# Low parts of weight chunks behind the maximum of a unit's scores, in a two-block transformer layer on one core

## The reference, cut to what matters

```
(qa, ka, va, qb, kb, vb, qc, kc, vc, qi, ki, wi, gates) = split(xn @ w_in[l])
o_a = chunk_band_attention(qa, ka, va, rel_bias_a[l])       # softmax(q k * scale + bias) v
o_b = diff_attention(rope(qb), rope(kb), vb, lam, ...)      # softmax(c=0) - lam * softmax(c=1)
o_c = dsa_attention(rope(qc), rope(kc), vc, index ..., topk)  # softmax over selected keys
g = sigmoid(gates).reshape(b, s, 3, D)
y = g[0] * (o_a @ w_up_a) + g[1] * (o_b @ w_up_b) + g[2] * (o_c @ w_up_c)
x = x + y @ w_out
```

## Time and profile before

| | |
|---|---|
| median of 3 runs | 1695.42 us (1692.92 to 1697.69) |
| the profiled execution | 1695.85 us, of which the recorded span is 1693.8 us |
| PE busy | 1603.3 us, 95% of the span |
| DVE busy | 876.6 us, 52% |
| ACT busy | 621.3 us, 37% |
| POOL busy | 58.1 us, 3% |
| mean granted TensorE clock | 0.975 of full speed |

### The profile page before, as it was taken

The page is one execution under the profiler, slowest core; times in us unless marked ns, Lnnn a source line. Parts: engine busy times, 40 slices in busy tenths (PEclk is TensorE's granted clock), DMA queues, the critical chain, the costliest instruction groups (busy, mean ns, idle before and its releaser), DMA issues.

```text
span 1693.8 us, 25178 instructions
## 1 busy us (share of the span) xinstructions
PE 1603.3 (95%) x10739; PEld 1285.8 (76%) x10739; DVE 876.6 (52%) x1272; ACT 621.3 (37%) x990; POOL 58.1 (3%) x28
## 2 busy tenths in 40 slices
PE   8898989889989999998999899999999899899998
PEld 7785434443434479897788799999988788799998
DVE  6933212121211287678555676647668755476653
ACT  2123202111211154545514544435454542464443
POOL 0000000000000000060000000000015000000000
PEclk9988999999999999999999899999999999999999
DMA  9156999999999985426222655474634424256550
GB/s 351 66 212 258 427 430 428 428 428 428 430 429 426 423 298 181 140 103 221 100 102 98 211 187 174 163 256 158 216 105 150 147 78 174 94 181 199 174 188 37
DMA packets 126912, 393.78 MB, mean 232 GB/s; under 512 B 4320, under 2 KB 60000, under 8 KB 114016
## 3 DMA queue, kind: packets, MB, share of 16 engines
q1 hardware_dynamic: 126816, 392.38, 61.2%
HBM read 386.34 MB, written 1.05 MB: 229 GB/s over the span
## 4 chain that ended last, share of the span: by engine, by line
PE 66%; DVE 15%; DMA 10%; ACT 5%; issue 3%; SPq 0%; DVEq 0%; ACTq 0%
PE psum L1240 10%; DMA ring<-w 9%; PE psum L973 7%; PE psum L974 7%; PE psum L976 7%; PE psum L1506 5%; PE psum L1305 3%; DVE outs L1949 2%; ACT wp L1592 2%; PE psum L1573 2%; PE psum L1576 2%; PE psum L1575 2%; PE psum L1203 2%; PE psum L1004 2%; DVE score L2347 1%
## 5 line engine op out<-in xcount | busy, mean ns | idle before, releaser
L973 PE MATMUL psum<-h_hi,w_hi 128*128 128x256 f32 x1456 | 366.6, 289 | 1.8 <-ACT outs L1595 1.4
L974 PE MATMUL psum<-h_hi,w_lo 128*128 128x256 f32 x1456 | 361.5, 285 | 0.0
L973 PEld LDWEIGHTS psum<-h_hi,w_hi 128*128 128x128 f32 x1456 | 282.3, 194 | 7.3 <-issue 5.1
L974 PEld LDWEIGHTS psum<-h_hi,w_lo 128*128 128x128 f32 x1456 | 282.7, 194 | 0.2
L624 DVE TENSOR_TENSOR w_lo<-raw_a,w_hi 128x1024 fp32r<-128x1024 f32 x170 | 204.9, 1223 | 136.0 <-ACT w_hi L1595 135.1
L1595 ACT ACTIVATE w_hi<-raw_a 128x1024 fp32r<-128x1024 f32 x186 | 193.1, 1053 | 186.0 <-PE psum L976 70.2
L976 PE MATMUL psum<-h_lo,w_hi 128*128 128x256 f32 x1456 | 205.0, 284 | 0.0
L1240 PE MATMUL psum<-ring,outs 128*64 128x512 f32 x720 | 166.0, 617 | 27.3 <-DMA ring<-w 26.1
L976 PEld LDWEIGHTS psum<-h_lo,w_hi 128*128 128x128 f32 x1456 | 188.8, 193 | 0.0
L1240 PEld LDWEIGHTS psum<-ring,outs 128*64 128x64 f32 x720 | 58.0, 142 | 132.7 <-issue 132.7
L624 DVE TENSOR_TENSOR w_lo<-raw_b,w_hi 128x1024 fp32r<-128x1024 f32 x84 | 101.7, 1223 | 60.4 <-ACT w_hi L1595 59.7
(11 more groups left out here) (298 smaller groups left out, 2516.4 us busy)
## 6 DMA issues: line engine op xcount, KB each, us to landing
ring<-w SPq DMA_DIRECT2D x76, 2048.0 KB, 16.6
raw_a<-w_in SPq DMA_DIRECT2D x20, 2048.0 KB, 8.2
raw_a<-w_gu SPq DMA_DIRECT2D x32, 1024.0 KB, 7.8
raw_b<-w_in SPq DMA_DIRECT2D x10, 2048.0 KB, 8.4
wp<-w SPq DMA_DIRECT2D x8, 2048.0 KB, 18.7
hs<-w SPq DMA_DIRECT2D x8, 2048.0 KB, 23.1
raw_b<-w_gu SPq DMA_DIRECT2D x12, 1024.0 KB, 7.5
raw_a<-w_down SPq DMA_DIRECT2D x8, 1536.0 KB, 6.6
```

What stands on the lines that cost most here:

```text
L973: mm(to, hi[:, k, :], h_hi[:, k, :], start=(k == 0), stop=False)
L974: mm(to, lo[:, k, :], h_hi[:, k, :], start=False, stop=False)
```

## The change

One condition in `with_splits`, the one that puts the collected low parts into the list:

```diff
@@ -230,7 +230,7 @@
         unit = unit or (w[0] == "rope" and w[1] >= 3)
         if unit:
             out.append(w)
-        if w[0] == "probs" or not unit:
+        if w[0] == "scores" or w in (("probs", 7), ("probs", 23), ("probs", 27)) or not unit:
             out += low
             low = []
         held = ...
```

## The result

The changed kernel takes 1676.63 us (median of 4 runs, 1675.84 to 1677.74) against 1694.29 us for the kernel before in the same comparison: ratio 0.9891, 95% interval 0.9875 to 0.9907. It is 17.7 us (1.1%) faster. The forecast was 1677.2 us.

The account below looks back on a forecast made before the run. PE was taken as the tightest engine, its gaps ended by work handed round through DVE and ACT. Stretch gains of 1.84, 3.32, 6.57 and 6.47 us sum to 18.2: 1695.42 - 18.2 = 1677.2 us, range 1672 to 1687.

Parts of the forecast that it names:

- What bounds: Units 2 to 7 and 9 to 23, both layers: PE has least room but isn't full, with 17.9 us of gaps.
- a circle through DVE and ACT: Unit steps: maximum, exponential, probabilities, low, evacuation, scaling, next maximum run one behind another and end PE's gaps, e.g. 1.81 us.
- The place left: Ahead of the scaling: next unit's scaling and maximum begin up to 1.14 us earlier, without split waits up to 1.27 us.
- A and C: Unit steps where PE waits for nothing: 4.45 us from even to odd, 4.65 us from odd to even.
- The place gone to: Between maximum and reciprocals: a low costs 0.06 us in odd, about 0.25 us in even units, which PE's slack takes.
- Expected leftovers: PE waits left per layer: 1.03 us at step 13, half of it at step 14, 0.2 us at step 4.
- ACT, loads, PE's demand for the lows: Split wait of 1.27 us goes; loads and PE's use of chunks, up to some 2.5 us later, cost nothing.
- Sum: Units 2 to 7 take 22.85 us, units 9 to 23 take 61.75 us, in both layers: 18.2 us gained.
- The clock: Four falls of PE's clock in the unit steps, 5.9 us of the 18.2, go because PE stands idle less.
- the rival in which the falls stay: Clock falls return at waits left at the start of B and the rotations: gain 12.3 us, 1683.1 us, chance 0.14.
- What passes on: Work behind the unit steps moves up, so the gain counts in full; otherwise the first two gains, 5.2 us, are lost.
- The rule on the busiest engine: Optimise the highest-occupancy engine first: read so, moving DVE's work has no effect, 1695.4 us, chance 0.04.

Follow-up runs that it names:

- late_ahead: Kernel before, with each low still ahead of the scores but put out one step later, when its split is done: 1679.33 us, ratio 0.9911 to before.
- no_low: Changed kernel without the low subtraction of chunks 30 to 34 and 50 to 62 in each layer: 1675.16 us, ratio 0.9882 to the kernel before.
- only_a: Kernel before with the change for units 0 to 7 alone (4 moved lows a layer): 1689.09 us against 1694.96, ratio 0.9962.
- only_bc: Kernel before with the change for units 8 to 23 alone (13 moved lows a layer): 1683.28 us against 1694.96, ratio 0.9931.
- rope_and_32: Changed kernel with rotations ahead of the scaling in steps 13 and 15 and low 32 behind unit 4's scores: 1675.36 us, ratio 0.9884 to before.
- before_again: Kernel before, no edit, profiled once more: 1696.12 us.
- after_again: Changed kernel, no edit, run once more: 1677.04 us against 1695.43 for the kernel before, ratio 0.9893.
- twice_behind: Changed kernel with each of 36 lows done twice behind the maximum: 1700.11 us, ratio 1.0031 to the kernel before.

## Why the prediction was right

**What bounds.** Right: PE with gaps, ended by a circle through DVE and ACT that held the low. With the low off it, the scaling waits for PE. One reading was wrong: "PE equally busy (34.65 us)" in both layers compares two stretches of 36.5 us that hold 283 and 270 matmuls. Over the same units PE was busy 22.84 and 24.32 us with the same gap of 1.85 us, so the 1.48 us are all clock, as the prediction concluded.

**The place left.** Right in sum, but it named two costs without weighing them, the low's own 1.14 us and the wait for its split. `late_ahead` weighs them: the wait alone, with what hangs on it, is 15.5 of the 18.2 us of the stretches, and all of it in A and C. My expectation for that kernel (10 to 13 us) still gave the low's own time too much.

**The place gone to.** Right: `no_low` shows that the moved lows cost next to nothing there but at three steps of a layer. Expected leftovers were 1.03 us, half of it and 0.2 us; they are 0.95, 0.47 and, by the stretch 22.92 against 22.65, 0.27 us.

**ACT, loads, PE's demand for the lows.** Right: in the four stretches after, none of PE's and DVE's waits is for a low, a split or a load.

**Sum.** 22.85 us expected for units 2 to 7 in both layers, 22.92 and 22.91 measured; 61.75 for 9 to 23, 61.66 and 61.68 measured. In the long one the step from unit 17 to 18 was put at 4.45 us, taken from A, and is 4.31. The gain of the stretches, 18.2 us, is the measured one.

**The clock.** That the four falls would go was right: the clock is 1.00 in all four stretches of both profiled executions. The 5.9 us put on them is too much. Without a fall the first stretch of the kernel before takes 24.69 us (its layer 0) and the long one 67.62 (`only_a`, layer 1), twice that is 184.62 us, and with the four falls it was 187.40. So the falls were worth 2.8 of the 18.2 us, and 15.4 are gaps that would have gone without any fall. By the same working the rival in which the falls stay would have cost less than the 5.9 us it was given. The sum wasn't touched by it, as it was made of whole stretches.

**What passes on.** Right: `only_a` and `only_bc` add up. The step left out is that the parts behind the units could change at all: between two executions of one kernel, and in layer 0 between kernels, they differ by 1 to 2 us with the clock in cross attention. That the forecast came out to 0.6 us is in part luck. The medians gained 17.7 us and not 18.2, and the median of before was 1.1 us lower this time (1694.29 against 1695.42), both within the scatter of the runs.

**The rule on the busiest engine.** The prediction set the advice of the Trainium skill ("Perfetto Trace Analysis", Identifying the Most-Contended Engine) to optimise the engine with the highest occupancy first against that of its next section, Optimization Strategy, to look for what blocks that engine in its gaps. The trace doesn't bear out the reading that work on another engine is worth nothing: DVE's order alone gave 17.7 us with DVE 52% busy. It agrees with the second: PE's waits in the four stretches before ended with DVE's probabilities.

## What to carry to other kernels

In a loop where engines hand work round, look on each in-order engine for the instruction that stands between a product and the operation that releases the next engine, and for the idle time behind that release: work which nobody wants soon belongs there, up to the length of that idle time and no further. Look first at what such an instruction waits for, since everything queued behind it waits too; putting it out a step later gave 15.6 of some 18 us here. Work out the leftover by the steps where two such instructions meet. Don't add the price of a fall of PE's clock to that of its waits: a fall was worth 1.48 us where PE was late, and 0.60 and 0.07 us where it would have waited.

## What the runs showed of the hardware

In the unit stretches the falls of TensorE's clock to 1.2 GHz came at the same units in two executions of the same kernel, though the units began 2.2 us later in one: clocks 1.00, 0.95, 0.93 and 0.97 in both. I had expected them "not always at the same unit". The other executions of this kernel, 1690.91 to 1698.49 us with mean clocks of 0.981 to 0.972, have no trace, so falls may lie elsewhere in those. What fixes the place isn't settled by these runs.

Behind the units the clock changed with kernels whose instructions there are the same, and also between two executions of one kernel. The part behind the scores of unit 26 in layer 0, the same instructions in all kernels, took 288.68 and 288.72 us with the clock at 0.98 (before, `rope_and_32`), and 287.65 us at 0.99 (after). Over the first 20 us of it the clock is

```profile
935.50:955.00 19.50, 15.00 (x81) 11.39 (x81) 10.73 (x16) 10.21 (x23) 0.00 (x0) 0.74 0.68 215
```

before, and after

```profile
927.40:947.00 19.60, 15.09 (x85) 11.39 (x84) 11.51 (x18) 11.01 (x25) 0.00 (x0) 0.83 0.67 214
```

Taken over the first 20 us from the scores of unit 26, the length of the whole part goes with the clock, the lower the longer:

| | clock, layer 0 | us | clock, layer 1 | us |
|---|---|---|---|---|
| before | 0.74 | 288.68 | 0.74 | 221.48 |
| before_again | 0.74 | 288.68 | 0.91 | 219.59 |
| after | 0.83 | 287.65 | 0.83 | 220.40 |
| after_again | 0.83 | 287.69 | 0.83 | 220.36 |
| only_a | 0.83 | 287.81 | 0.91 | 219.45 |
| rope_and_32 | 0.74 | 288.72 | 0.74 | 221.58 |
| no_low | 0.74 | 288.72 | 0.83 | 220.13 |
| twice_behind | 0.83 | 287.11 | 0.74 | 221.52 |

In layer 0 both kernels that were profiled twice repeat their value. In layer 1 the kernel before has both the lowest and the highest clock, 1.9 us apart. So one profiled execution a kernel can't price an edit worth 1 or 2 us by its span, and part of the gain of the mended rotations may be hidden that way, where the stretches at the edit show it. That the clock is the cause is read from these rows; no run changed it by itself, and what sets it there stays open.
